# The first pass of an expert loop: one indirect transfer of whole rows, turned by TensorE, in place of four quarter-row transfers turned by VectorE

## The reference

```python
scores = sigmoid(h @ w_router)                       # 64 experts, top 8 of the best 4 groups of 8
act    = silu(h @ w1[e]) * (h @ w3[e]) * gate[e]     # 1024 -> 256, for the 8 chosen experts
routed = sum over the chosen e of act @ w2[e]        # 256 -> 1024
shared = (silu(h @ ws1) * (h @ ws3)) @ ws2           # one expert that every token uses
out    = x + gate2 * rmsnorm(routed + shared)
```

## Time and profile before

| | |
|---|---|
| median of 3 runs | 1256.03 us (1255.23 to 1256.8) |
| the profiled execution, own time | 1263.06 us |
| its span | 1261.3 us |
| PE busy | 1185.5 us, 94% |
| POOL, DVE, ACT busy | 523.8, 556.3, 334.6 us |
| PE's granted clock, mean | 0.973 of full speed |
| DMA, mean over the span | 268 GB/s |

### The profile page before, as it was taken

One profiled execution on the slowest core, in us unless ns is written; L12 is line 12 of the kernel. 1 busy time (PEld: TensorE's weight loads), 2 busy tenths in 40 slices (PEclk: granted clock), 3 DMA queues, 4 the chain that ended last, 5 costly groups with the idle time before them and its releaser, 6 DMA issues.

```text
span 1261.3 us, 25647 instructions
## 1 busy us (share of the span) xinstructions
PE 1185.5 (94%) x8947; PEld 847.3 (67%) x8948; DVE 556.3 (44%) x902; ACT 334.6 (27%) x631; POOL 523.8 (42%) x527
## 2 busy tenths in 40 slices
PE   5799999999999899977989999998989999899997
PEld 4599999999999899965844544554445544455542
DVE  0566685667668868216733232222122222122134
ACT  4432322322323452335211111111111111111122
POOL 1154444444448344410554544453334544434420
PEclk9799999999999899998989999999999999899999
DMA  9954344344421233407979999999999999999997
GB/s 295 292 174 134 114 150 150 108 124 150 150 84 46 70 89 95 134 1 316 357 279 380 388 362 411 407 410 410 411 410 408 412 406 392 407 409 407 348 339 272
DMA packets 160222, 337.43 MB, mean 268 GB/s; under 512 B 14734, under 2 KB 99290, under 8 KB 143776
## 3 DMA queue, kind: packets, MB, share of 16 engines
q1 hardware_dynamic: 140096, 295.55, 62.9%
q0 software_dynamic: 16656, 34.14, 7.2%
q10 hardware_dynamic: 3424, 7.09, 1.8%
HBM read 322.21 MB, written 33.30 MB: 282 GB/s over the span
## 4 chain that ended last, share of the span: by engine, by line
PE 72%; DMA 9%; SPq 6%; issue 6%; DVE 5%; POOL 1%; ACT 1%; DVEq 0%; ACTq 0%; POOLq 0%
PE ps L1707 23%; PE ps L1718 12%; PE ps L1469 10%; PE ps L1470 9%; PE ps L1471 9%; DMA w<-in_w_dram 4%; SPq L343 3%; PE ps L1713 2%; DMA ring<-in_w_ada_dram 2%; SPq L348 1%; PE ps L1482 1%; PE ps L1424 1%; DMA act<-y_rows 1%; SPq L303 1%; DVE sg L1126 1%
## 5 line engine op out<-in xcount | busy, mean ns | idle before, releaser
L1707 PE MATMUL ps<-w,xe 128*64 x3136 | 365.9, 387 | 18.8 <-DMA w<-in_w_dram 13.3
L1707 PEld LDWEIGHTS ps<-w,xe 128*64 128x64 f32 x3136 | 224.5, 139 | 156.7 <-issue 54.7
L518 POOL TENSOR_TENSOR wsplit<-ring,wsplit 128x1024 fp32r<-128x1024 f32 x80 | 194.7, 2434 | 291.1 <-ACT wsplit L719 278.6
L1469 PE MATMUL ps<-h_s_hi,wsplit 128*128 128x260 f32 x960 | 272.3, 284 | 0.0
L1471 PE MATMUL ps<-h_s_hi,wsplit 128*128 128x260 f32 x960 | 270.8, 282 | 0.0
L1470 PE MATMUL ps<-h_lo_m_hi,wsplit 128*128 128x260 f32 x832 | 234.7, 282 | 0.0
L1345 DVE TENSOR_TENSOR rs<-sg,ps 128x128 f32<-128x128 f32 x98 | 28.1, 287 | 389.5 <-issue 263.9
L1718 PE MATMUL ps<-w,eactT 128*64 (+1 forms) x784 | 189.2, 603 | 7.2 <-issue 6.1
L1469 PEld LDWEIGHTS ps<-h_s_hi,wsplit 128*128 128x128 f32 x960 | 180.6, 188 | 6.7 <-issue 5.9
L1471 PEld LDWEIGHTS ps<-h_s_hi,wsplit 128*128 128x128 f32 x960 | 180.8, 188 | 0.0
L719 ACT ACTIVATE wsplit<-ring 128x1024 fp32r<-128x1024 f32 x80 | 84.7, 1059 | 296.8 <-PE ps L1471 286.5
(11 more groups left out here) (323 smaller groups left out, 1325.7 us busy)
## 6 DMA issues: line engine op xcount, KB each, us to landing
w<-in_w_dram SPq DMA_DIRECT2D x192, 1024.0 KB
ring<-in_w_in_dram SPq DMA_DIRECT2D x56, 512.0 KB, 3.9
ring<-in_w_ada_dram SPq DMA_DIRECT2D x12, 2048.0 KB
ring<-y_rows SPq DMA_DIRECT2D x4, 2048.0 KB, 12.6
ring<-in_w_out_a_dram SPq DMA_DIRECT2D x8, 512.0 KB, 4.1
ring<-in_w_out_b_dram SPq DMA_DIRECT2D x8, 512.0 KB, 4.1
ring<-in_w_o_dram SPq DMA_DIRECT2D x8, 512.0 KB, 4.1
act<-y_rows SPq DMA_DIRECT2D x2, 2048.0 KB, 14.9
```

What stands on the lines that cost most here:

```text
L518: pool.tensor_tensor(wsplit[:, b, 1], raw[raw_slot], wsplit[:, b, 0], ALU.subtract).then_inc(S["w_lo"], 1)
L1469: mm(ps[:, bank + h, 0:HT], wsplit[:, b, 0, k, :], hi[:, k, p:q], start=(k == 0), stop=False)
L1707: ins = mm(ps[a * STRIP:(a + 1) * STRIP, 2 + f, 0:2 * P], xe[:, k, a * STRIP:(a + 1) * STRIP], w[a][:, k, :, f * P:(f + 1) * P], start=(k ...
```

## The change

For pass 0 alone, the four quarter-row transfers become one indirect transfer of whole rows (4 KB each). Its row numbers are one column of the places, taken straight from PSUM by a new one-column DVE instruction ahead of the copy to `tok1`. `idx_dve` therefore counts one more, and every wait for it is one higher. The transfer is issued before POOL waits for `idxG`.

PE turns the rows itself: eight transposes into banks 4 and 5 between `shared_up(1, 1, 0)` and `shared_up(1, 1, 1)`. They read every eighth channel of a row, which is the order of the channels that the experts' weights use. ACT copies bank 4 and DVE bank 5 into `xe`, both behind the last `shared_up`. PE waits for both copies before the first expert. `gather(1, 1)` and all later passes stay as they were. The counts of two semaphores are adapted (`gcopy`, and `xg_in[0]`, which pass 0 now raises by 16 and not by 64). PE takes the first slot's address from a constant and not from the table.

```diff
@@ gpsimd @@
             pool.wait_ge(rows_out[1], 16 * 2)
-            pool.wait_ge(S["idx_dve"], 2)
-            pool.wait_ge(g2_out, 16)
             last_row, last_y = pool.alloc_register("last_row"), pool.alloc_register("last_y")
+            pool.reg_mov(last_row, T - 1)
+            pool.wait_ge(S["idx_dve"], 1)
+            pool.indirect_dma_start(out=xgs[0], out_offset=None, in_=h2_rows,
+                                    in_offset=bass.IndirectOffsetOnAxis(ap=sidx[:, 5:6], axis=0),
+                                    bounds_check=last_row, oob_is_err=False).then_inc(xg_in[0], 16)
             pool.reg_mov(last_row, 4 * T - 1)
...
-                pool.wait_ge(S["gcopy"], p + 1)
+                pool.wait_ge(S["gcopy"], p)
...
-            gather(0, 0)
+            pool.wait_ge(S["idx_dve"], 3)
+            pool.wait_ge(g2_out, 16)
             shared_gated(1)
@@ scalar @@
+            act.wait_ge(S["idx_pe"], 2)
+            act.activation(flat(xe[:, 0:4, :]), ps[:, 4, :], ACT.Copy).then_inc(S["xe_dve"], 1)
             act.wait_ge(S["sh_act"], 2)
+            act.wait_ge(S["xe_dve"], 2)
@@ vector @@
             dve.wait_ge(S["idx_mm"], 1)
+            link(ts(sidx[:, 5:6], ps[:, 7, 0:1], -1.0, None, ALU.add), "idx_dve", wait=False)
             link(dve.tensor_copy(tok1[:, :], ps[:, 7, 0:JOBS]), "idx_dve", wait=False)
...
             dve.wait_ge(S["sh_mm"], 2 * FT)
-            for h in range(2):
-                rows_T(0, 64, h)
+            dve.wait_ge(S["idx_pe"], 2)
+            dve.tensor_copy(flat(xe[:, 4:8, :]), ps[:, 5, :]).then_inc(S["xe_dve"], 1)
...
-                    rows_T(1 - u, it * 64 + 64 * (u + 1), f)
+                    rows_T(1 - u, it * 64 + (64, 80)[u], f)
@@ tensor @@
-            pe.wait_ge(S["idx_dve"], 1)
+            pe.wait_ge(S["idx_dve"], 2)
...
             shared_up(1, 1, 0)
+            pe.wait_ge(S["idx_dve"], 3)
+            pe.wait_ge(xg_in[0], 16)
+            v = xgs[0].rearrange("s (m c) -> s c m", c=C)
+            for c in range(C):
+                ins = tr(ps[:, 4 + c // 4, (c % 4) * P:(c % 4 + 1) * P], v[:, c, :], ident[:, :])
+            mark(ins, "idx_pe")
             shared_up(1, 1, 1)
...
-            pe.reg_load(next_at, first_at[0:1, 0:1])
+            pe.reg_mov(next_at, slot_at[1])
...
             pe.wait_ge(S["early_dve"], 2)
+            pe.wait_ge(S["xe_dve"], 2)
```

## The result

The changed kernel takes 1264.62 us (median of 6 runs, 1263.78 to 1268.02) against 1256.41 for the kernel before, run beside it (6 runs, 1255.23 to 1260.56): ratio 1.0063, 95% interval 1.0047 to 1.008. On two later occasions it was 1.0041 both times (1.0024 to 1.0059 and 1.0027 to 1.0054), so the loss is 5 to 8 us. The forecast was +2.0 us, and 1261.0 us at most. All ratios and intervals here are of a kernel against the kernel before that ran beside it.

A forecast was written before the change was run, and what follows sets the result against it. PE's own work, 72% of the span, was taken to bound the kernel. The last `shared_up` ending 7.45 us later, less 5.49 from there to the second pass, gave +1.96: 1258.0 us, range 1251.2 to 1261.0.

The forecast's parts named there:

- The rest is counted at nothing: Other effects on POOL, DVE, SP's later transfers, the extra DVE instruction and the constant: taken as no change in time.
- The landing: New whole-row transfer for pass 0: starts at 622.1, takes 8.3 us, lands at 630.4, range 625.4 to 631.2.
- ceiling of 631.2: Latest landing of pass 0's rows, if served behind all 3 MB of weights: 3.6 MB at 408 GB/s, 8.9 us from 622.
- rival C: Row transfer served last: landing 631.2, idle 5.4, clock loss 2.6, change +3.5, 1259.5 us; chance 0.30.
- The clock loss: PE's slower clock after 4.6 us idle between the `shared_up` halves: 1.9 us, bounds 0 and 2.6.
- landing + clock loss - 630.35: Short form of the forecast's sum for the whole change; landing + clock loss was forecast at 632.3, the change at +1.96.
- The transposes' stride: PE's eight new transposes read with a stride of eight elements: taken as 0.87 us, ceiling twice that.
- From E to the first product: ACT's and DVE's work and copies between the last `shared_up` and the first expert product: 1.5 us, clock unchanged.
- E: The moment the last `shared_up` ends: 629.45 before, forecast 636.9 after, 7.45 us later.
- The second gather: In the first pass, the next rows come 1.85 late, PE stalls 1.97 us; second pass starts at E + 14.63.
- Carried one to one: A shift of PE near 640 us was taken to reach the kernel's end in full, since weights follow PE's passes.
- Rival D: The saturated stretch from 750 us on swallows the shift, so nothing arrives at the end: 1256.0 us; chance 0.03.

The follow-up runs named there:

- e3: Changed kernel with expert 4's weights issued only when the rows of pass 0 have landed; 1262.1 us, ratio 1.0029.
- e18: Changed kernel with 239 unexecuted instructions at the head of PE's program, timed once more in a later group; 1259.71 us, ratio 1.0023.
- e11: Changed kernel with 239 unexecuted instructions at the head of PE's program, first timing; 1263.18 us, ratio 1.0029.
- e0: The kernel before, unchanged, for a second trace; 1260.13 us, ratio 1.000.
- e16: The kernel before with 256 unexecuted instructions (16 KB) at the head of PE's program; 1257.81 us, ratio 1.0007.
- e13: Changed kernel, weights after rows, 239 unexecuted instructions, and PE's wait for the rows' first half left to the loop's own; 1258.37 us, ratio 0.999.
- e4: Changed kernel with only PE's wait for the rows' first half left to the loop's own; 1266.37 us, ratio 1.0052.
- e12: Changed kernel with expert 4's weights held until pass 0's rows land, plus 239 unexecuted instructions at the head of PE's program; 1257.7 us, ratio 0.9994.
- e17: The changed kernel as it is, for a third trace; 1262.32 us, ratio 1.0041.
- e15: The kernel before with 17 unexecuted instructions at the head of PE's program; 1260.38 us, ratio 1.0028.
- e7: The changed kernel as it is, for a second trace; 1262.94 us, ratio 1.0041.
- e10: Changed kernel with expert 4's weights held until pass 0's rows land, plus 239 instructions executed at three upstream waits; 1265.11 us, ratio 1.0062.
- e9: Changed kernel with 239 more instructions in PE's program, executed at three upstream waits; 1269.14 us, ratio 1.0091.

## Why the prediction was wrong, step by step

**The step that failed most is one that it didn't have.** "The rest is counted at nothing" went through POOL, DVE and SP, but not through PE's own program. Seventeen added instructions shift the loop's code, and ahead of the first pass behind its first jump back PE then stands still for 1.1 to 3.0 us. That it waits for instructions there is inferred, from the extra fetch of q8; the gap itself has no releaser. Measured by itself the place of the code is 2.6 us, a third to a half of the loss, and more than the whole forecast change.

**The landing was sized too short.** The transfer started at 619.95, R + 0.6; the forecast of 622.1 was R + 1.1. It landed at 630.0, 10.1 us later, where I had 8.3 and a ceiling of 631.2, R + 10.2. Relative to R the landing is R + 10.7, past rival C. The cause was right: SP had asked for 2 MB at 619.42 and for the third at 620.27, and with these held back (e3) it took 4.6 us. (So the low end of 3.3 us, from a scatter, was too short as well.) The ceiling had the bytes right, 3.57 MB of rows and weights moved from 619.95 to 630.05, but I divided them by the steady rate of 408 GB/s; the mean was 353, with only 188 in the first 2 us. Rival C's reason, rows served last, did not hold: q0 stood behind q1 for more than four us and then shared with it, as the scatter of 676.88 had.

**The clock loss** followed: 5.79 us idle (forecast 4.6) cost 1.94 + 5.24 less what the same work takes at full clock (1.13 + 3.67 in e3), that is 2.4 us (forecast 1.9, bound 2.6). The bound compared a time of the timeline (8.62) with one of the chain (6.04); the timeline has 6.21 for the same product at full clock, which makes the loss before 2.4 as well. The idle time alone does not give the loss: after 4.57 us (e18) it was 1.5, after 4.70 (e11) 2.8, and in the old order 1.6 after 5.70 (e0) and 2.8 after 5.43 (e16). The prediction's short form, landing + clock loss - 630.35, gives with the landing put on before's R (630.0 + 1.7) 631.7 + 2.4 - 630.35 = +3.75. The second pass moved by 3.7. So the frame of the sum held up to the second pass, and its two terms were short by 1.3 and 0.5.

**The transposes' stride** cost little: 1.13 us in e3 at full clock against 0.87.

**From E to the first product** took 2.6 us (637.07 to 639.63), forecast 1.5. Both copies ended by 638.26; PE began 1.4 us later, at a gap marked issue. With the wait inside the loop it is 0.7 us less (e13), so about half of this belongs to the wait that stands outside of the loop. Taking it away gained nothing in the second pass, as e13 and e4 showed, because of the next step. That the clock stays through such a gap was right here (6.26 us for the product), but in e3, e12 and e18 the same gap of 2.4 us was followed by a product of 7.95.

**The second gather** was right: the second pass starts E + 14.3 to E + 14.4 in the three traces of the changed kernel, forecast E + 14.63, and DVE waits for conv's rows (3.25 us). The forecast stall of 1.97 was shared between the later entry and the 0.50 us in front of `act_T(1)`.

**Carried one to one**: e18 is 3.1 us behind e16 at the second pass, 3.1 at pass 8, 3.9 at the last, and 1.9 us in time (1259.71 against 1257.81), with about 2 us to either side. The other pair, e17 against e15, has 4.0 at the second pass, 3.4 at pass 8, 4.0 at the last, and 1.9 us in time. In the traces the shift reaches the last pass whole; the times are too coarse to confirm or refute it. Rival D, that nothing arrives, is contradicted by these traces and by e15 and e16, where 2.1 us at pass 8 are 3.1 at the last.

**The sum as it should have been**: +3.7 at the second pass and +2.6 for the code's place, +6.3 us; measured were +8.2, +5.4 and +5.1. The two terms overlap somewhat, since the place also moved the landing. By the medians of the last group, which hold both, the change costs 1.9 us at either place of the code and the place 2.6, together 4.5. That 1.9 is next to the forecast's 2.0 is luck: its landing and its clock loss were both short, and each difference has about 2 us to either side.

Rows first and the code in place (e12) undo both, and the time is back at before's (0.9994). Its second pass leads by only 1.3 us because of the second gather, which lands late there as in e3:

```profile
638.11 1.09 DVE L1334 STREAM_TRANSPOSE xe<-conv 128x512 f32<-128x512 f32 x1 [4.22 <-DMA conv<-h_rows,gidx]
```

That the time does not win even the 1.3 has its reason in the passes: 1 to 4 take 11.2 to 11.9 us each in e12, and at pass 4 the lead over e0 is 0.6, at pass 8 0.2. What holds these passes up was not tried.

**Open.** Whether PE lacks a chunk of code at the jump, and which, and why 17 instructions decide it, the traces don't show: they date the fetches but don't name their addresses. Also open is why passes 5 to 18 take 11.16 us each in some executions and mostly 11.16 and 11.6 by turns in others. This goes with the group that ran together and not with the kernel: 11.16 in e7 to e10, e15 to e18 and the first trace of the changed kernel, by turns in e0 to e3, e11 to e13, e4 and the first trace of the kernel before. PE's waits for weights go with it too, 20.8 to 25.4 us in the first kind and 13.3 to 17.6 in the second. So from pass 8 on only traces of one kind can be compared.

## What to carry to other kernels

Adding instructions ahead of a long unrolled loop moves its code, and that alone can cost microseconds (2.6 here). Before a small change is judged, put unexecuted instructions into the old kernel until its loop lies where the new one's does, or into the new one until it lies a whole 16 KB further. A transfer that must land within a few microseconds should be asked for ahead of the bulk weights, not behind them (4.6 against 10.1 us here); but look at what the weights then meet, for here it was the next rows, and the time did not improve on before. The wait for such a transfer belongs where nothing else is queued behind it. And a landing worked out from the steady rate of full queues (408 GB/s) is no ceiling: here the mean was 353.

## What the runs showed that I had not expected

- Seventeen instructions that never run cost 2.6 us (e15 against e16).
- The same 128-row transfer took 4.6 to 5.0 us with the weights held back (e3, e10, e12, e13), and behind 3 MB of weights 9.8 to 10.1, or 8.9 to 9.2 with 256 more instructions in PE's program.
- Moving a wait earlier made a pass slower: in e13 PE idled 3.29 us ahead of `act_T(1)` in place of 1.45 and lost 2.5 us of clock behind it.
- A wait on a long-reached semaphore is not free: 239 instructions of them at three places where PE had 4 us or more to spare moved R by 7 to 10 us (e9 against the three traces of the changed kernel).
- PE needs about 1.4 us from the last copy's end into the loop when it is released outside it, and 0.7 less when the wait stands inside.
